# A hybrid diffusion step on one core: attention's head pairs in the order latent, prompt, latent, prompt

## What is computed

```python
def attn_context(h, ...):
    s = einsum('bqkgd,bskd->bkgqs', qg, k) * HEAD_DIM ** -0.5
    p = softmax(concatenate([s, s_sink], -1))[..., :L]
    o = einsum('bkgqs,bskd->bqkgd', p, v)
    return o @ wo, k, v

def attn_latent(h, k_ctx, v_ctx, ...):
    s_loc = einsum('bnqkgd,bnskd->bnkgqs', qb, k_band) * scale
    s_ctx = einsum('bnqkgd,bckd->bnkgqc', qb, k_ctx) * scale
    p = softmax(concatenate([s_loc, s_ctx, s_sink], -1))
    o = einsum(p_loc, v_band) + einsum(p_ctx, v_ctx)
    return o @ wo
```

## Time and profile before

| | us |
|---|---|
| median of 3 runs | 1290.28 (1289.5 to 1290.41) |
| the profiled execution's own time | 1290.15 |
| its span, first to last instruction | 1288.3 |
| attention from scores(0) to the projection's start | 711.6 to 750.2 |
| projection (L645) in the chain that ended last | 750.35 to 777.98 |
| granted TensorE clock | 1.00, which is 2.4 GHz |

### The profile page before, as it was taken

The page is one execution under the profiler, slowest core; times in us unless marked ns, Lnnn a source line. Parts: engine busy times, 40 slices in busy tenths (PEclk is TensorE's granted clock), DMA queues, the critical chain, the costliest instruction groups (busy, mean ns, idle before and its releaser), DMA issues.

```text
span 1288.3 us, 18829 instructions
## 1 busy us (share of the span) xinstructions
PE 1259.3 (98%) x6948; PEld 700.5 (54%) x6948; DVE 442.9 (34%) x1499; ACT 326.3 (25%) x723; POOL 56.7 (4%) x86
## 2 busy tenths in 40 slices
PE   6999999999999999999999899999999999999998
PEld 3876775545555445444454568554455445544544
DVE  1696272222222222222244736322222222222223
ACT  3575331122122212221131623222112211221211
POOL 0295000000000000000000000000000000000000
PEclk9999999999999999999999999999999999999999
DMA  9987999999999999999998796799999999999994
GB/s 363 382 325 298 405 414 391 411 419 419 421 420 421 421 420 421 421 420 418 411 366 364 146 378 236 293 406 419 419 420 421 420 420 421 421 420 421 420 419 193
DMA packets 84071, 497.43 MB, mean 386 GB/s; under 512 B 10729, under 2 KB 19601, under 8 KB 27696
## 3 DMA queue, kind: packets, MB, share of 16 engines
q1 hardware_dynamic: 83440, 496.47, 95.0%
q10 hardware_dynamic: 576, 0.22, 0.1%
HBM read 493.26 MB, written 3.41 MB: 386 GB/s over the span
## 4 chain that ended last, share of the span: by engine, by line
PE 86%; DVE 6%; DMA 4%; ACT 2%; issue 1%; SPq 0%; POOL 0%; ACTq 0%; DVEq 0%
PE ps L972 34%; PE ps L1004 17%; PE ps L1015 10%; PE ps L943 7%; PE ps L645 4%; DVE ps L1617 3%; PE ps L737 3%; DMA ring<-in_conv_w_dram 2%; PE ps L886 2%; DMA S<-in_exp_w_up_dram 2%; PE ps L613 2%; PE ps L990 1%; PE ps L927 1%; PE ps L982 1%; PE ps L633 1%
## 5 line engine op out<-in xcount | busy, mean ns | idle before, releaser
L972 PE MATMUL ps<-ring,xg 128*64 128x512 f32 x1344 | 296.8, 593 | 0.2
L972 PEld LDWEIGHTS ps<-ring,xg 128*64 128x64 f32 x1344 | 104.6, 137 | 186.7 <-issue 167.9
L972 PE MATMUL ps<-S,xg 128*64 128x512 f32 x704 | 154.9, 592 | 0.2 <-DMA S<-in_exp_w_up_dram 0.2
L1004 PE MATMUL ps<-ring,W 128*64 128x512 f32 x672 | 153.4, 598 | 0.0
L1910 DVE TENSOR_TENSOR ypart<-ps,ypart 128x512 fp32r<-128x512 f32 x128 | 88.5, 692 | 179.6 <-ACT ypart L1439 179.6
L1899 DVE SCALAR_TENSOR_TENSOR vec<-silu_h,W,ps 128x256 f32<-128x256 f32 x64 | 30.8, 481 | 333.2 <-ACT silu_h L1433 333.2
L1015 PEld LDWEIGHTS ps<-comb,ypart 128*128 128x128 f32 x1024 | 126.4, 190 | 18.6 <-issue 18.6
L1015 PE MATMUL ps<-comb,ypart 128*128 128x256 f32 x1024 | 135.2, 285 | 0.0
L1433 ACT ACTIVATE silu_h<-ps 128x256 f32<-128x256 f32 x64 | 24.6, 384 | 407.3 <-PE ps L972 407.3
L1428 ACT ACTIVATE xg<-ps 128x384 f32<-128x384 f32 x176 | 83.2, 491 | 168.3 <-PE ps L943 168.3
L1439 ACT ACTIVATE ypart<-ps 128x512 fp32r<-128x512 f32 x128 | 76.4, 597 | 184.7 <-PE ps L1004 184.7
(11 more groups left out here) (251 smaller groups left out, 1083.7 us busy)
## 6 DMA issues: line engine op xcount, KB each, us to landing
ring<-in_exp_w_gate_dram SPq DMA_DIRECT2D x86, 1024.0 KB, 15.7
ring<-in_exp_w_up_dram SPq DMA_DIRECT2D x86, 1024.0 KB, 18.6
ring<-in_exp_w_down_dram SPq DMA_DIRECT2D x86, 1024.0 KB, 18.4
S<-in_exp_w_gate_dram SPq DMA_DIRECT2D x44, 1024.0 KB, 16.1
S<-in_exp_w_up_dram SPq DMA_DIRECT2D x44, 1024.0 KB, 19.4
S<-in_exp_w_down_dram SPq DMA_DIRECT2D x44, 1024.0 KB, 18.7
ring<-in_ada_w_dram SPq DMA_DIRECT2D x26, 1024.0 KB, 20.3
S<-in_ada_w_dram SPq DMA_DIRECT2D x22, 1024.0 KB, 14.2
```

The source lines that it names most:

```text
L972: mm = pe.matmul(PGU[64 * b:64 * b + 64, :].rearrange("p (h f) -> p h f", h=2), xg[:, places[k][m], 64 * b:64 * b + 64], gate_up_of(w[b])[ ...
L1004: mm = pe.matmul(bank[64 * b:64 * b + 64, :], hidT[:, j, 64 * b:64 * b + 64], down_of(w[b])[:, j, n * 512:(n + 1) * 512], start=(j == 0), ...
```

## The change

`HEADS` is interleaved: items (1,0), (1,1), (0,0), (0,1), (1,2), (1,3), (0,2), (0,3). Pair 1 becomes a prompt pair and pair 2 a latent pair: L, P, L, P in place of L, L, P, P. The number of instructions of each form stays; so do SP's and POOL's programs. `TURNED` and the waits that depended on the old order follow.

```diff
-        HEADS = [(1, j) for j in range(NKV)] + [(0, j) for j in range(NKV)]
+        HEADS = [(1 - g, 2 * p + b) for p in range(NKV // 2) for g in range(G) for b in range(2)]
-        TURNED = [2 * (i + 1) if i < NKV else NKV + i + 1 for i in range(2 * NKV)]
+        TURNED = [sum(1 + HEADS[n][0] for n in range(i + 1)) for i in range(2 * NKV)]
...
                         k0 = 0 if g == 0 else T
-                        if m in (0, NKV // 2):
+                        if m < 2:
                             pe.wait_ge(at_trc, 4 if m == 0 else 7)
...
-                            pe.wait_ge(at_ptc, TURNED[i - 1 if i <= NKV else i - 2])
+                            pe.wait_ge(at_ptc, TURNED[i - 1 if nk == 2 or i % 2 == 0 else i - 2])
...
                         exps(2 * m + 1)
-                        if m < NKV // 2:
+                        if HEADS[2 * m][0]:
                             context_copy(2 * m)
                             context_copy(2 * m + 1)
```

## The result

The changed kernel takes 1293.59 us (median of 10 runs, 1292.37 to 1295.18), against 1290.56 for the kernel before on the same chip (10 runs, 1289.50 to 1292.63): 3.0 us more, a ratio of 1.0022 with a 95% interval of 1.0015 to 1.0030. The forecast was 1291.3 and the range ended at 1292.8. The direction, slower by a little, is that of the walk; the size is three times as large as the walk's 1.06.

What follows compares the result with a forecast made beforehand. Attention was taken as bound by handing on between TensorE, VectorE and ScalarE, with no engine full. Round differences -0.86 + 0.0 + 1.92 gave +1.06 us on 1290.15, so 1291.2, adjusted to 1291.3; range 1289.5 to 1292.8.

Steps and rivals of the forecast that it cites:

- the walk: Attention stage: following the engines' queues with measured durations, round by round; +1.06 us at the stage's end.
- Rounds 1 and 2: Attention, between ends of exps(2m+1): first 8.4 us instead of 9.26, second 8.3, the same as before.
- Round 3: Attention, from the end of exps(5) to that of exps(7), prompt after latent pair: 8.65 us instead of 6.73.
- The hole: Attention: TensorE idle from the end of values(1) to transposes(4), 2.15 us; longest before 1.27.
- the third mark: Attention: end of exps(7), the last pair's second exponentials, at 747.10 us instead of 746.05.
- the order's whole cost: Attention's three round differences summed: -0.86 + 0.0 + 1.92 = +1.06 us.
- a delay arrives at the end: Behind attention, dry DMA slices wait for TensorE, so the long weights' stream shifts whole, by 1.06 us.
- the rival of the clock: Attention: after TensorE's 2.15 us idle the clock falls from 2.4 to 1.2 GHz, giving 1303 or 1331 us; chance 0.04.
- the rival of the better overlap: Attention: a prompt pair's short steps fill TensorE's idle time in a latent pair, 1287.0 us or less; chance 0.03.

Runs made afterwards that it cites:

- outer_latent: Changed kernel with the pairs in the order L, P, P, L; 1293.49 us, ratio 1.0022.
- again: Changed kernel measured and profiled once more, nothing altered; 1294.38 us, ratio 1.0025.
- look2: Changed kernel, nothing altered, profiled a fourth time; one run, 1293.66 us.
- unit_in_hole: Changed kernel with unit EARLY + 12 moved from behind transposes(4) to in front of them; 1291.74 us, ratio 1.0008.
- hole_before: Kernel before with unit EARLY + 13 moved from behind transposes(5) to behind values(2); 1290.90 us, ratio 1.0002.
- both_moves: Changed kernel with unit EARLY + 12 in front of transposes(4) and output_copy(m) behind exps(2m+3); 1289.75 us, ratio 0.9989.

## Why the prediction missed

**Step by step.** Rounds 1 and 2: 730.21 and 738.52 against 730.1 and 738.5, right, with their reasons (values(0) behind its unit at 726.14 against 726.05; the second round over scores, maxima and exponentials). Round 3: its working was right as long as the clock stays. The hole was there (2.13 against 2.15), and with the hole filled the third mark lies 27.10 us behind transposes(0), where the forecast's 747.10 makes 27.08; the order's whole cost was then 1.07 against 1.06. That a delay arrives at the end: right, 2.51 at the experts' first long piece against 2.50 at values(3), and the time follows the stage within 0.7 us for every kernel of the table (outer_latent by its projection).

**The step that failed** is in the rival of the clock, which was given 0.04: "the eight matmuls of 512 columns behind it took 1.93, which is full speed". It isn't. Eight matmuls of the same shape take 1.06 in the earlier trace rows, at 741.10; 1.93 is what they take at 1.2 GHz, as in the run again at 739.82, where the clock reads 0.50. I had read the clock's column, 1.00, and not the row's duration against its own kind. So the clock was put at nothing in the sum, and the runs showed 1.43 to 2.86 us for it. In the changed kernel the launch's start has the same 1.93, there with a column that says so:

```profile
15.53 1.93 PE L613 MATMUL ps<-S,scT 128*32 128x512 f32 x8 [2.94 <-DMA S<-in_ada_w_dram]
12.00:16.00 4.00, 1.06 (x12) 0.20 (x8) 0.00 (x0) 3.24 (x10) 0.00 (x0) 0.75 1.02 398
16.00:20.00 4.00, 4.00 (x14) 2.16 (x7) 0.00 (x0) 0.00 (x0) 0.00 (x0) 0.50 1.02 394
```

The row that I had used to shut the rival out says nothing against it: behind the hole of 2.11 us the matmuls ran at half speed in the kernel before too. It doesn't show either that such a hole makes the clock fall, for the group in front of that hole had already run at half speed:

```profile
11.54 1.93 PE L613 MATMUL ps<-S,scT 128*32 128x512 f32 x8 [1.21 <-DMA S<-in_ada_w_dram]
```

Read rightly, the row would have left the chance of 0.04 without its reason. How likely the fall was could not be told from it; with the fall the forecast would have been 1.4 us higher or more.

**The rival's price was wrong as well**: 11.9 or 40 us, where the runs show 1.43 to 2.86. I let the clock stay low to the end of the stage or beyond; it came back 3.5 to 6 us after transposes(4) had begun, while TensorE was working. With this price the rival gives 1292.7 to 1294.2, from just inside the range's end of 1292.8 to past it, instead of far outside. (In the rival of the better overlap a sum is off as well: a gain beyond 2.58 us means 1287.7 or less, not 1287.0.)

**The last part**: 1.06 and a clock's 1.4 to 1.6 make 2.5 to 2.7, and the medians differ by 3.0 and 3.6. The intervals, 1.9 to 3.9 and 1.9 to 4.6 us, include 2.5, so no further cost is shown; falls as dear as the 2.86 of again would add to the median, but only four runs have a profile. The last weights' transfer took 19.9 to 21.1 us in the profiles whose chain ends with it, in no order that follows a change (20.78 in the changed kernel, 20.09 in again, 21.09 in look2, 19.89 in outer_latent); I have no cause for that.

## What to carry to other kernels

Where no engine is full, walk the queues with measured durations before trusting that an exchange of equal pieces costs nothing: where the clock stayed at 2.4 GHz, the walk gave values(3) to 0.3 us in every order here, and its best order gained 3.7 us with the same instructions. In that walk look for TensorE's longest hole, and treat one that is longer than any in the kernel before as a risk to the clock. Judge the clock by the duration of a matmul against the same form elsewhere, not by the clock's column alone; work that nothing waits for, like the units here, belongs into the hole.

## What the runs showed that I had not expected

- A hole of 2.13 us was followed by transposes at half speed in all four profiles of the changed kernel; holes of 1.13 (unit_in_hole), 1.27 (before) and 1.68 (hole_before) were not. What lies between was not tried in this stage. Nor is the fall tied to the hole's end: at the launch's start of both_moves a hole of 2.26 was followed by a unit of 1.14, near full speed, and most of the fall in the clock's column came behind that unit (0.62 from 16 to 20 us).
- What a fall costs differs from execution to execution, 1.43, 1.60, 1.62 and 2.86 us. The times don't show it as a wider spread: 2.8 us over ten runs of the changed kernel, 3.1 over ten of the kernel before.
- The clock's column can read 1.00 over matmuls at half speed: in the profile of before 1.00 with 1.93 us for eight matmuls of 512 columns, in that of the changed kernel 0.50 with the same 1.93.
